# Both borders of w_up in a hybrid GLA and MLA decoder block: first token half split during w_out, sums and the last low part on GpSimd, last pair's convolution and first f tiles in another order

## The reference, cut to what matters

```
mixed = (sigmoid(gate_a) * y_gla + sigmoid(gate_b) * y_mla) @ w_out     # 1024 x 1024
h     = layernorm(ALPHA * x + mixed, ln1_g, ln1_b)
u     = h @ w_up                                                        # 1024 x 5632
u     = causal depthwise conv of width 3 over tokens (conv_w), + conv_b
f     = (silu(u[:, :2816]) * u[:, 2816:]) @ w_down                      # 2816 x 1024
out   = layernorm(ALPHA * h + f, ln2_g, ln2_b)
```

## Time and profile before

| | us |
|---|---|
| median of 3 executions | 1921.3 |
| lowest, highest | 1920.02, 1930.49 |
| profiled execution, own time | 1929.85 |
| its span | 1928.1 |
| PE busy | 1845.5 (96%) |
| DVE, ACT, POOL busy | 862.9, 639.4, 780.7 |

### The profile page before, as it was taken

One profiled execution on the slowest core, in us unless ns is written; L12 is line 12 of the kernel. 1 busy time (PEld: TensorE's weight loads), 2 busy tenths in 40 slices (PEclk: granted clock), 3 DMA queues, 4 the chain that ended last, 5 costly groups with the idle time before them and its releaser, 6 DMA issues.

```text
span 1928.1 us, 23389 instructions
## 1 busy us (share of the span) xinstructions
PE 1845.5 (96%) x9124; PEld 1544.4 (80%) x9124; DVE 862.9 (45%) x1426; ACT 639.4 (33%) x1166; POOL 780.7 (40%) x571
## 2 busy tenths in 40 slices
PE   8999999999999999999989999699999999899995
PEld 6888888888888988788867888578888888688884
DVE  2324342342501136454455533665544554566447
ACT  2313232232300153554452102654444544221122
POOL 3222122122222333233333366277767776244344
PEclk9999999999999999999999999799999999899998
DMA  5111212023344116422343443122322231744422
GB/s 179 44 45 42 68 45 88 22 83 126 104 135 133 45 55 233 147 79 80 102 127 124 149 159 125 66 88 74 97 82 77 77 99 56 296 151 144 173 98 88
DMA packets 178281, 202.52 MB, mean 105 GB/s; under 512 B 16317, under 2 KB 129133, under 8 KB 178173
## 3 DMA queue, kind: packets, MB, share of 16 engines
q1 hardware_dynamic: 144332, 139.94, 22.5%
q10 hardware_dynamic: 33840, 61.10, 9.1%
HBM read 149.10 MB, written 51.90 MB: 104 GB/s over the span
## 4 chain that ended last, share of the span: by engine, by line
PE 87%; DVE 6%; ACT 3%; issue 1%; POOL 1%; DMA 1%; SPq 0%; ACTq 0%; DVEq 0%; POOLq 0%
PE psum_all L785 25%; PE psum_all L787 25%; PE psum_all L786 25%; PE psum_all L1009 1%; PE psum_all L1025 1%; PE psum_all L824 1%; PE psum_all L1026 1%; PE psum_all L1027 1%; PE psum_all L862 1%; PE psum_all L858 1%; DVE pT_lo L1207 1%; PE psum_all L860 1%; PE psum_all L997 1%; PE psum_all L998 1%; PE psum_all L995 1%
## 5 line engine op out<-in xcount | busy, mean ns | idle before, releaser
L699 POOL CAST w_hi<-w_raw 128x512 fp32r<-128x512 f32 (+8 forms) x117 | 116.9, 999 | 774.6 <-PE psum_all L787 714.1
L701 POOL TENSOR_TENSOR w_lo<-w_raw,w_hi 128x512 fp32r<-128x512 f32 (+8 forms) x117 | 279.9, 2392 | 9.5
L785 PE MATMUL psum_all<-xT_hi,w_hi 128*128 128x512 f32 (+1 forms) x528 | 212.5, 403 | 1.6 <-DVE xT_lo L1207 1.6
L787 PE MATMUL psum_all<-xT_hi,w_lo 128*128 128x512 f32 (+1 forms) x528 | 209.0, 396 | 0.0
L786 PE MATMUL psum_all<-xT_lo,w_hi 128*128 128x512 f32 (+1 forms) x528 | 209.0, 396 | 0.0
L785 PE MATMUL psum_all<-t_hi,w_hi 128*128 128x512 f32 x352 | 138.5, 393 | 5.8 <-DVE t_lo L1207 3.0
L743 POOL TENSOR_TENSOR w_lo<-s_sb,w_hi 128x512 fp32r<-128x512 f32 x88 | 112.7, 1293 | 71.2 <-ACT w_hi L2033 71.2
L786 PE MATMUL psum_all<-t_lo,w_hi 128*128 128x512 f32 x352 | 138.0, 392 | 0.0
L787 PE MATMUL psum_all<-t_hi,w_lo 128*128 128x512 f32 x352 | 137.9, 392 | 0.0
L785 PE MATMUL psum_all<-w_hi,xT_hi 128*128 128x256 f32 (+2 forms) x448 | 126.3, 282 | 0.0
L786 PE MATMUL psum_all<-w_lo,xT_hi 128*128 128x256 f32 (+2 forms) x448 | 125.2, 279 | 0.0
(11 more groups left out here) (477 smaller groups left out, 4417.5 us busy)
## 6 DMA issues: line engine op xcount, KB each, us to landing
w_raw<-in_w_up_dram SPq DMA_DIRECT2D x44, 512.0 KB, 3.9
f_raw<-d_f SPq DMA_DIRECT2D x44, 512.0 KB, 3.6
w_raw<-in_w_in_dram SPq DMA_DIRECT2D x16, 1024.0 KB, 5.2
d_f<-up_g SPq DMA_DIRECT2D x44, 256.0 KB, 3.4
w_raw<-in_w_down_dram SPq DMA_DIRECT2D x22, 512.0 KB, 4.7
w_raw<-in_w_out_dram SPq DMA_DIRECT2D x8, 1024.0 KB, 5.0
x_tok<-in_x_dram SPq DMA_DIRECT2D x8, 512.0 KB, 6.6
w_raw<-in_w_in_dram SPq DMA_DIRECT2D x8, 512.0 KB, 5.5
```

The lines of the kernel that those rows point to most:

```text
L699: wc.done(nc.gpsimd.tensor_copy(w_hi[b][:, w], w_raw[b][:, w]))
L701: low = nc.gpsimd.tensor_tensor(w_lo[b][:, w], w_raw[b][:, w], w_hi[b][:, w].bitcast(F32), ALU.subtract)
L785: pe.matmul(out_ap, ah, bh, start=start and i == 0, stop=False, skip_group_check=more)
L787: last = pe.matmul(out_ap, al, bh, start=False, stop=stop and i == len(terms) - 1, skip_group_check=more)
```

## The change

- The first token half is transposed inside w_out: feature tiles 0 to 3 behind the third token tile of slot 5 (j == 4), into banks 0 to 3, and tiles 4 to 7 behind the third of slot 6 (j == 5), into the same banks. Slot 7 (j == 6) waits for `h_lo` of the tile that lay in its bank. `rows_low` is cut into `rows_affine` and `rows_low`; DVE and ACT make b11 and b21 during slots 5 to 7.
- POOL makes S1 of pair 0 first, then the four low parts of A11 and A12, then S2 and S4, the low parts of S1, and S3.
- In pair 0 S3 goes before S2; T3 is made for all four tiles before T2; `t4_low` leaves DVE and becomes a POOL subtraction (`t_pool`), after POOL's 14 low parts of pair 0. ACT's order follows. DVE makes `add_u2` and `add_u3` of each u behind the first two gate convolutions.
- TensorE's first A12 product is cut in two halves with transposes around them.
- Last pair: `f_high(0)` and `f_low(0)` come ahead of the last `add_u2`; the value's second half is convolved first, without its first two tokens (`end_conv_main`), these two (`end_conv_seam`) and the first half (`end_conv_first`) later, with `f_low(1)` ahead of them; ACT makes `f_high(1)` before A22 is read.
- Memory: b11 and b21 move to the region of h_tok's far half, f_raw to where b11 and b21 then lie; up_g, up_v and others move. `f_load` waits for the stores of the first four pairs instead of all but the last.

```
-        t2_lo = a("t2_lo", ...)   # and r12, up_g, up_v, p1_sb, p5_sb, u2_sb: from region A to region R
+        b11_hi = a("b11_hi", [P, QK, HALF], F32R)   # b11, b21: from region R to region A
...
-        ln1_gt = a("ln1_gain", [P, D])
+        f_raw = [a(f"f_raw{i}", [P, S]) for i in range(8)]
...
+        FIRST = ("A11", "A12", "S1", "S4", "S3", "S2", "A22")
+        OTHER = ("A11", "A12", "S1", "S4", "S2", "S3", "A22")
...
# SP
             sp.wait_ge(sm["up_mm"], PRODUCTS - 10)
             for u in range(2):
-                sp.wait_ge(f_out[u], 32 * (PAIRS - 1))
+                sp.wait_ge(f_out[u], 32 * 4)
             for q in range(8):
                 f_load(q)
             for u in range(2):
-                for half in range(2):
+                sp.wait_ge(f_out[u], 32 * (PAIRS - 1))
+            for u in range(2):
+                for half in (1, 0):
                     f_store(PAIRS - 1, u, half)
...
# POOL
+            for u in range(2):
+                pool.wait_ge(upg_in[u], 16)
+                s1_sum(0, u)
+            for g in range(4):
+                up_low(g)
+            for u in range(2):
+                s24_sums(0, u)
+            for u in range(2):
+                up_low(place(0, "S1", u))
+            for u in range(2):
+                s3_sum(0, u)
+            for g in range(6, 14):
+                up_low(g)
+            for j in range(QK):
+                pool.wait_ge(*act_made("t4_hi", j))
+                nc.gpsimd.tensor_tensor(t4_lo[:, j, :], r21[:, j, :], t4_hi[:, j, :].bitcast(F32), ALU.subtract).then_inc(sm["t_pool"], 1)
+            for m in range(1, PAIRS):
...
# TensorE, w_out
-                    if th == 1 and not second:
-                        pe.wait_ge(sm["wo_ev"], 4 * dh + t - 3)
+                    if j == 4:
+                        pe.wait_ge(sm["wo_ev"], t - 3)
+                    if j == 6:
+                        pe.wait_ge(*dve_made("h_lo", t))
...
-                if j == 6:
-                    pe.wait_ge(sm["wo_ev"], 12)
-                    pe.wait_ge(sm["ln_n"], 4)
-                    for k in range(4):
-                        rows_t(0, k, 4 + k)
+                    if j == 4 and t == 6:
+                        pe.wait_ge(sm["wo_ev"], 8)
+                        pe.wait_ge(sm["ln_n"], 4)
+                        for k in range(QK):
+                            rows_t(0, k, k)
+                    if j == 5 and t == 6:
+                        for k in range(QK):
+                            pe.wait_ge(*dve_made("h_lo", k))
+                            rows_t(0, QK + k, k)
...
# TensorE, entry
+            product(0, "A11", 0)
+            product(0, "A11", 1)
             pe.wait_ge(sm["wo_ev"], 16)
             pe.wait_ge(sm["ln_n"], TT)
             rows_t(1, 0, 1)
+            rows_t(1, 1, 5)
             rows_t(1, 4, 2)
             rows_t(1, 5, 6)
             rows_t(1, 6, 3)
             rows_t(1, 7, 7)
             pe.wait_ge(sm["snap"], 1)
+            product(0, "A12", 0, (0, 1))
             pe.wait_ge(*dve_made("t1_lo", 0))
             rows_t(1, 2, 1)
+            product(0, "A12", 0, (2, 3))
             pe.wait_ge(*dve_made("t1_lo", 1))
             rows_t(1, 3, 5)
+            pe.wait_ge(sm["snap"], 2)
+            product(0, "A12", 1)
...
+                        if what == "S3" and m == 0:
+                            pe.wait_ge(*dve_made("t4", u))
+                        if what == "S2" and m == 0:
+                            pe.wait_ge(*dve_made("t4", 2 + u))
+                        if what == "A22":
+                            if m == 0:
+                                pe.wait_ge(sm["t_pool"], QK)
+                            pe.wait_ge(*u_made(m, "c22", u))
...
# DVE
-            out_rows(1, 0)
-            for k in range(QK):
-                rows_low(k)
+            rows_affine(0)
+            rows_affine(1)
+            rows_low(0)
+            rows_affine(2)
+            rows_low(1)
+            rows_affine(3)
+            rows_low(2)
+            rows_low(3)
+            out_rows(1, 0, (0, 1, 2))
+            rows_affine(4)
+            rows_affine(5)
+            rows_low(4)
+            rows_affine(6)
+            rows_low(5)
+            rows_affine(7)
+            out_rows(1, 0, (3,))
+            rows_low(6)
+            rows_low(7)
             out_rows(1, 1)
-            for k in range(QK, KT):
-                rows_low(k)
...
+                    if m == PAIRS - 1:
+                        f_low(0)
+                    add_u2(m, 0)
...
+            end_conv_main(0)
+            f_low(1)
+            end_conv_seam(0)
+            end_conv_first(0)
+            end_conv_main(1)
+            end_conv_seam(1)
+            end_conv_first(1)
...
# ACT, last pair
-                    if k == 12 and m == PAIRS - 1:
+                    if k == 8 and m == PAIRS - 1:
                         ac.wait_ge(sm["up_mm"], PRODUCTS - 6)
                         f_high(0)
...
-            value_id(PAIRS - 1, 1, 0)
-            value_id(PAIRS - 1, 1, 1)
+            for u in range(2):
+                end_value_id(u, 1)
+            ac.wait_ge(sm["up_mm"], PRODUCTS - 2)
+            f_high(1)
+            for u in range(2):
+                end_value_id(u, 0)
             ac.wait_ge(sm["up_mm"], PRODUCTS)
```

More of the change, by code:

```diff
@@ L241, in block_kernel @@
         t4_hi = a("t4_hi", [P, QK, HALF], F32R)
[L242 to L248, removed]
+        b11_hi = a("b11_hi", [P, QK, HALF], F32R)
+        b11_lo = a("b11_lo", [P, QK, HALF], F32R)
+        b21_hi = a("b21_hi", [P, QK, HALF], F32R)
+        b21_lo = a("b21_lo", [P, QK, HALF], F32R)
         r = Region(R0, RSZ)
@@ L253, in block_kernel @@
         t3_lo = r("t3_lo", [P, QK, HALF], F32R)
[L254 to L257, removed]
+        up_g = [[r(f"up_g{u}{half}", [P, HALF]) for half in range(2)] for u in range(2)]
+        up_v = [r(f"up_v{half}", [P, HALF]) for half in range(2)]
+        p1_sb = [r(f"p1_sb{u}", [P, HALF]) for u in range(2)]
+        p5_sb = [r(f"p5_sb{u}", [P, HALF]) for u in range(2)]
+        u2_sb = [r(f"u2_sb{u}", [P, HALF]) for u in range(2)]
+        r12 = nc.alloc_sbuf_tensor_at("r12", [P, QK, HALF], F32, offset=R0 + 56 * KB)
+        t2_lo = r("t2_lo", [P, QK, HALF], F32R)
         t4_lo = r("t4_lo", [P, QK, HALF], F32R)
@@ L354, in block_kernel, with order, place @@
         PRODUCTS = 14 * PAIRS
-        OPERANDS = ("A11", "A12", "S1", "S4", "S2", "S3", "A22")
+        FIRST = ("A11", "A12", "S1", "S4", "S3", "S2", "A22")
+        OTHER = ("A11", "A12", "S1", "S4", "S2", "S3", "A22")
+        def order(m):
+            return OTHER if m else FIRST
+        def place(m, what, u):
+            return 14 * m + 2 * order(m).index(what) + u
         def ring(g, lo=False):
@@ new lines, in _ @@
+                        if what == "A11":
+                            if m == 0:
+                                continue
+                            pe.wait_ge(sm["g_c"], 4 * m - 1 + u)
+                        if what == "A12":
+                            if m == 0:
+                                continue
+                            pe.wait_ge(sm["snap"], 4 * m + u + 1)
+                        if what == "S1":
+                            if m:
+                                pe.wait_ge(sm["f_ok"], 4 * m - 2 + 2 * u)
+                            else:
+                                pe.wait_ge(*dve_made("t1_lo", QK - 1))
@@ L1166, in down @@
+                        product(m, what, u)
             def down(i, t):
@@ L1622, in add_u2, with end_conv_first @@
+            def end_conv_first(u):
+                m = PAIRS - 1
+                ve.wait_ge(sm["f_ok"], 4 * m + 2 * u + 1)
+                ve.wait_ge(sm["g_si"], 4 * m + u + 1)
+                vc.done(taps(u2_sb[u][:, :], up_bank(u, 1), 4 * u + 2, 0, FT + 2 * m + u))
+                vc.wait()
+                V.tensor_tensor(up_g[u][0][:, :], up_g[u][0][:, :], up_bank(u, 1), ALU.mult).then_inc(sm["f_ok"], 1)
             def add_u2(m, u):
-                ve.wait_ge(sm["up_mm"], 14 * m + 9 + u)
+                ve.wait_ge(sm["up_mm"], place(m, "S2", u) + 1)
@@ L2078, in gate_silu, with end_value_id @@
                 A.activation(up_g[u][half][:, :], up_g[u][half][:, :], ACT.Silu).then_inc(sm["g_si"], 1)
+            def end_value_id(u, half):
+                m = PAIRS - 1
+                fc = FT + 2 * m + u
+                if half:
+                    ac.wait_ge(*u_made(m, "c22", u))
+                    ac.wait_ge(sm["v_c"], 4 * m - 1 + u)
+                else:
+                    ac.wait_ge(sm["up_mm"], 14 * m + 13 + u)
+                A.activation((up_v if half else u2_sb)[u][:, :], up_bank(u, 2 + half), ACT.Identity, bias=cw[:, 3, fc:fc + 1],
+                             scale=cw[:, 2, fc:fc + 1]).then_inc(sm["v_id"], 1)
             def value_id(m, u, half):
```

326 lines of the change are left out of this document (175 added, 151 removed).

## The result

The changed kernel takes 1904.8 us (median of 4, 1903.1 to 1907.8) beside 1925.1 for the kernel before (median of 4, 1920.0 to 1930.5): ratio 0.9899, 95% interval 0.9875 to 0.9923. Forecast were 1908.6 us and a range of 1894 to 1917. Run again later beside other kernels it gave 0.9900 (0.9877 to 0.9923). The profiled execution has a span of 1903.2 us, 24.9 less than the one before.

What follows compares the result with a forecast made beforehand. TensorE, 96% busy, was taken as the bound, so time counts only at its waits at w_up's entry and exit: -18.5 + 5.8 = -12.7 us, from the median 1921.3 to 1908.6, range 1894 to 1917.

Steps and rivals of the forecast that it cites:

- Transposes in w_out, no charge: In w_out: 32 moved transposes find their inputs ready, w_out still ends at 1204.1; nothing charged, at worst a few tenths.
- Pair 0, 25.0 us earlier: Entry of w_up: the first pair of products ends at 1249.4 instead of 1274.4 us, most waits gone or shorter.
- Not all of it stays: Pair 1's third product waits 4.1 us for ACT's snapshot behind GpSimd's late sum; 20.8 us gained, not 25.0.
- 2.3 us for the clock behind it: Half clock charged after the 4.1 us wait ahead of pair 1's third product: 2.3 us lost.
- the entry: Start of w_up: 20.8 us gained less 2.3 for slow clock, -18.5; bounds -21.5 and -14.
- The last A22: End of w_up: DVE's early f low parts cause a new 4.1 us wait; w_up ends 5.4 us late, bounds 3 and 8.
- Slot 2: Third w_down weight slot, split only at 1692.2: TensorE idles 8.0 us, the next 18 matmuls cost 2.8 more.
- The exit: From w_up's end into w_down: slot 2 ready at 1692.2 instead of 1689.2, plus 2.8: +5.8; bounds -9.7 and +9.
- The sum: Whole kernel: -18.5 at the start of w_up and +5.8 at its end, -12.7 us, giving 1908.6.
- (c): Rival, chance 0.07: TensorE stays at half clock through pair 0's short waits; slower, +5 to +10 us, up to 1931.
- (a): Rival, chance 0.22: w_up's exit gains too, slot 2 lands in time, A22 not held up; 1891, or 1898 with half.
- (b): Rival, chance 0.21: w_up's entry gives half, -11, through tighter ACT and DVE alternation and clock drops; exit +5, total 1915.

Runs made afterwards that it cites:

- slot 2 early: Changed kernel, but SP loads slot 2 of w_down behind the first eight f tiles, ahead of the last stores; ratio 0.9881 to the kernel before.
- the reload late: Changed kernel, but ACT issues the loads of ln gains and h only when slot 2 of w_down has landed; ratio 0.9885 to the kernel before.

## Why the prediction was right

- **Transposes in w_out, no charge.** Right: no wait from the start of w_out to pair 0, and the stretch from the first matmul on mT, ahead of w_out, to pair 0's first product is 186.5 us before and 186.2 after.
- **Pair 0, 25.0 us earlier.** Measured 25.4 (70.3 us from its first product to the end of its last before, 44.9 after). The waits left were put at 1.5, 1.1, 0 and 1.1 us; they are 1.36, 0.69, 0 and 0.34.
- **Not all of it stays.** Right in place, cause and size: the third product of pair 1 waits for ScalarE's copy behind GpSimd's sum, 2.91 us for 4.1. It starts 53.4 us behind pair 0's first product instead of 75.7: 22.3 gained for 20.8. The reason given for GpSimd's lateness, T4's low parts, was wrong: without them it begins no earlier.
- **2.3 us for the clock behind it.** Mis-sized in this trace, where it stayed at 1.00 (5.6 us for 24 matmuls); in the second trace of the same kernel it cost 1.6. This and the 1.5 us above are why the entry gave 22.2 and not 18.5. The reading that a wait of 3.00 us is the shortest with this effect was wrong in its own trace: there the clock also fell to 0.50 behind waits of 1.09 us, at 272 and 385 us.
- **The last A22.** Predicted 4.1 us of wait, measured 2.28 and in the second trace 3.40. The second low part was put at 2.06 us beside GpSimd's cast. It took 1.23 in the first trace, where GpSimd's cast took 2.04 instead of 1.04, and 1.97 in the second. From S4 on, w_up ended 4.2 us later than before the change, for 5.4 predicted.
- **Slot 2.** Predicted 8.0 us of idle and 2.8 of slow clock; measured 7.70 and 2.2, and 5.25 us of idle in the second trace. TensorE took slot 2 1.1 us later behind S4 than before the change, for 3.0 predicted. The exit came 4.9 us longer for 5.8, but by luck that close: 1.6 of the 4.9 lie in w_down's tail, where the same wait of 2.29 us was followed by slow clock after and not before, and the prediction had no such term.
- **The sum.** -12.7 forecast, -17.3 in the traces' two stretches, (0.9899 - 1) x 1925 = -19.4 in the times. So the mechanism was right and the gain too small by a third. That 1904.8 lies only 3.8 us from 1908.6 is partly luck: the median shown of before, 1921.3, was of three executions, and with the fourth (1920.0, 1921.3, 1928.8, 1930.5) it is 1925.05, from which -12.7 gives 1912.3. Two small slips in the working change nothing: slot 2's split took 4.8 us by the earlier trace rows, not 4.6, and rival (c) with the exit at its bound of +9 comes to about +8, not +10.
- **The rivals.** (a) did not happen: TensorE waited both at A22 and at slot 2. What it hoped for at slot 2 needs another order: with slot 2 early or the reload late the exit is 9.0 to 10.7 us shorter than the changed one. (b) and (c) did not happen either.

The rule weighed in the prediction (the Trainium skill, DMA: Bandwidth & Descriptors, "Issuing engines are not separate DMA queues") bears on what decided the exit. The trace agrees with 0.43 beside 0.41 MB in 2 us, and with ScalarE's reload moved behind slot 2 it landed in 7.1 us instead of 14.8.

## What to carry to other kernels

Follow a late transfer back to what shares the engines of DMA with it, not only to its place in its own queue: here slot 2's landing followed the start of another queue's reload, and the cure was one load issued earlier. When work is moved to an engine that is "free", ask what that engine waits for; GpSimd had 5 us of idle time ahead of its sums, so its new work cost nothing and taking it away gave nothing. And where two stages are changed at once, time each alone: the good half hid a loss of 0.46%.

## What the runs showed of the hardware

- **The length of a short wait doesn't tell whether half clock follows.** In 14 traces there are 19 waits between 1.9 and 3.6 us ahead of a product of w_up at the two borders. Behind 11 of them the next 24 matmuls kept full speed, behind 8 the granted clock went to 0.50 (1.2 GHz), 1.6 us lost, or 2.7 behind both waits of 3.00 us and one of 3.49. The same kernel did both at the same place: behind 2.91 us full speed, in the second trace behind 2.92 us half speed. What decides it is open. The drops near 272 and 385 us are of this kind too: each follows a wait of 1.09 us that the changed kernel's trace has as well, without a drop. One window of 2 us, first trace, then second (the clock is the third figure from the end):

```profile
1252.00:1254.00 2.00, 2.00 (x11) 1.65 (x10) 1.45 (x3) 0.62 (x1) 2.00 (x2) 1.00 1.05 368
```
```profile
1252.00:1254.00 2.00, 2.00 (x6) 1.52 (x6) 1.42 (x2) 0.00 (x0) 2.00 (x2) 0.50 1.05 367
```

- **Of VectorE and GpSimd the one that started later paid.** Two operations on SBUF met ahead of the last A22. Changed kernel, first trace: VectorE's low part starts at 1614.75 and takes 1.23 us, GpSimd's cast starts at 1614.84 and takes 2.04. Second trace: the cast starts at 1616.39 and takes 1.20, the low part starts at 1616.69 and takes 1.97. The two meet there in nine traces. In the five where VectorE starts first, or in the same hundredth, its low part takes 1.22 or 1.23 us, the cast 2.02 to 2.13, and TensorE waits 2.26 to 2.36 us at the last A22; in the four where GpSimd starts first, by 0.1 to 0.5 us, the low part takes 1.97 to 2.01, the cast 1.04 to 1.37, and TensorE waits 3.25 to 3.58. Rows of the first trace, VectorE and then GpSimd:

```profile
1614.75 1.23 DVE L1259 TENSOR_TENSOR f_1l<-f_raw,f_1h 128x1024 fp32r<-128x1024 f32 x1
```
```profile
1614.84 2.04 POOL L725 CAST w_hi<-w_raw 128x1024 fp32r<-128x1024 f32 x1 [8.99 <-PE psum_all L838]
```
